# FFN input product of a transformer step by one level of Strassen's scheme, output product as a phase of its own

## The chip, the core and the metric

The kernel runs on one NeuronCore of a Trainium2 chip. The metric is the device time of one execution in microseconds. All arrays are fp32; matmuls take their operands as fp32r, and each fp32 product is made of three fp32r products.

## What is computed

One layer of a hybrid backbone for 1152 tokens (1024 latent, 128 context), D = 1024: an input projection, attention, a gated recurrence, a merge, an output projection with a gated residual, and then the gated feed-forward (FFN) part with which this case deals. Cut to that part:

```python
def conv_glu(h, w_ffn_in, conv_w, conv_b, w_ffn_out):
    T = h.shape[1]
    gate, val = jnp.split(h @ w_ffn_in, 2, axis=-1)        # 1024 x 5632
    pad = CONV_W // 2
    gp = jnp.pad(gate, ((0, 0), (pad, pad), (0, 0)))
    gconv = conv_b + sum(gp[:, j:j + T] * conv_w[j] for j in range(CONV_W))
    return (jax.nn.gelu(gconv) * val) @ w_ffn_out          # 2816 x 1024

    x = x + gt1 * (mix @ lw['w_out'])
    h2 = rmsnorm(x, lw['g_ffn']) * (1.0 + sc2) + sh2
    x = x + gt2 * conv_glu(h2, ...)
y = rmsnorm(x, g_final)
```

## The kernel before

Every operand of a product is split into `hi` (its fp32r rounding) and `lo` (the rest); a product is hi x hi + hi x lo + lo x hi, so every step of 128 in the contraction is three matmuls. ACT makes `hi` by a copy, POOL (in some places DVE) makes `lo` by a subtraction.

Only `stage_out_ffn` (L2312) changes. It writes out the queue of each engine by hand: `sync` (SP, which issues the DMAs in order), `tensor`, `scalar`, `vector`, `gpsimd`. All stages follow one another in one block, and each engine works its queue in order; semaphores join the engines.

The stage's first part is the output projection (L2654): 9 token tiles x 2 halves (`o_unit`), 24 matmuls of 512 columns a unit. Behind each tile DVE gates it (L2798), adds the residual (L2801), takes squares (L2803) and normalises (L2808); PE transposes the tile (L2666), DVE applies gain and shift (`affine`, L2818) into `y`, ACT copies to `h_hi` (L2488) and POOL makes `h_lo` (L2581). `TRANSPOSED_AFTER` says behind which unit a tile's transposes stand. `h_hi` and `h_lo` hold h2 with features on the partitions and 1152 token columns.

Then come 11 pairs (`PAIRS`) of FFN chunks of 128 channels. For each pair PE makes the gate product of both chunks, 3 banks of 384 columns each (`gate_bank`, L2674, 24 matmuls a bank), the output product of the pair before (`outs`, L2707: 18 units of 6 matmuls of 512 columns), and the value product of both chunks (`value_chunk`, L2674). ACT takes the gate out of PSUM (L2504), DVE runs the width-3 convolution over it (L2828, L2832), ACT applies gelu (L2509), DVE multiplies by the value product in PSUM (L2840), and ACT and POOL split the result `u` (L2515, L2589) into SBUF tiles that the output product reads. DVE adds each pair's output product to `yacc` in SBUF (L2850, L2853). Weights come through `WeightStream` (L116 load, L124 hi, L129 lo), w_ffn_out through `load_w2` (L2413), `w2_split` (L2527, L2595). The last two pairs' output products are kept in PSUM and joined at the end: DVE gates them with gt2 (L2895), adds `yacc` (L2908), ACT squares (L2573) and takes the root, DVE scales (L2901), SP stores (L2471).

Of the kernel before, what the change touches and what calls it, by code (L numbers as in the profile page):

```python
# [21 lines left out]
P = 128  # L22
# [2262 lines left out]
PAD = NT + 4  # L2285
LAT0, CTX0 = 1, TL + 3
WO_RING, X_RING = 2, 3
HALF = D // 2
O_UNITS = 2 * TILES
TRANSPOSED_AFTER = (6, 7, 8, 9, 11, 13, 15, 17)  # L2290


def flat_pieces(j):

    if j < 2:
        return [(LAT0 + j * CH, j * CH, CH)]
    return [(LAT0 + 2 * CH, 2 * CH, TL - 2 * CH), (CTX0, TL, TC)]


def gate_order(g):  # L2300

    if g == 0:
        return [(0, 0), (0, 1), (1, 0), (1, 1), (0, 2), (1, 2)]
    return [(x, j) for x in range(2) for j in range(NCH)]


def gate_count(g, x, j):

    return 6 * g + gate_order(g).index((x, j)) + 1


def stage_out_ffn(nc, io, cst, sems, psum, base, m_hi, m_lo, h_hi, h_lo, home, merge):  # L2312
    sems.prefix = "s8"
    after_h = base + 2 * KD * NT * 4

    first = Arena(nc, after_h)
    WO_HERE = KD // 2
# [15 lines left out]
    late = Arena(nc, after_h)  # L2333
    yacc = late("yacc", [P, TILES, D])
    over = Arena(nc, first.at)
    g_base = over.at
    gpad = [over(f"gate_pad{i}", [P, PAD]) for i in range(2)]
    conv = [over(f"conv{i}", [P, PAD]) for i in range(2)]
    w2_raw = over("w2_raw", [P, 2, D])
    gt2_once = over("gt2_once", [P, D])  # L2340
    x1_back = [over("x1_back3", [P, HALF])]
    assert over.at <= HIGH - 8
    w2_hi, w2_lo = late("w2_hi", [P, 2, D], F32R), late("w2_lo", [P, 2, D], F32R)
    u_hi, u_lo = late("u_hi", [P, 2, NT], F32R), late("u_lo", [P, 2, NT], F32R)
    x1_back = [late(f"x1_back{i}", [P, HALF]) for i in range(3)] + x1_back
    assert late.at <= first_end


    gate_home = Arena(nc, g_base)
    u0_hi, u0_lo = gate_home("u0_last_hi", [P, NT], F32R), gate_home("u0_last_lo", [P, NT], F32R)  # L2350
    assert gate_home.at <= g_base + 2 * PAD * 4
    raw_home = Arena(nc, w_base)
    w2e_hi = raw_home("w2_last_hi", [P, 2, D], F32R)
    w2e_lo0 = raw_home("w2_last_lo0", [P, D], F32R)
    raw_home("w_hi1_kept", [P, D], F32R)
    w2e_lo1 = raw_home("w2_last_lo1", [P, D], F32R)

    end = Arena(nc, base)
    u1_hi, u1_lo = end("u1_last_hi", [P, NT], F32R), end("u1_last_lo", [P, NT], F32R)
    gt2 = [end(f"gt2_row{g}", [P, D]) for g in range(2)]  # L2360
    gfin = end("g_final_row", [P, D])
    x2 = [end(f"x2_{i}", [P, D]) for i in range(3)]
    fin = [end(f"final_rows{i}", [P, D]) for i in range(3)]
    assert end.at <= after_h
# [21 lines left out]
    win = io["w_ffn_in"].rearrange("(k p) n -> p k n", p=P)
    wout = io["w_ffn_out"].rearrange("(k p) n -> p k n", p=P)
    group = lambda t: 0 if t < TILES - 1 else 1
    LAST = PAIRS - 1
    Y_PAIRS = PAIRS - 2  # L2390
    Z_TILES = (TILES - 1,) + tuple(range(TILES - 1))

    def sync(sp):
        def load_wo(k):
            n = k - WO_HERE
            if n >= WO_RING:
                sp.wait_ge(wo_lo_ready, n - WO_RING + 1)
            sp.dma_start(wo_raw[n % WO_RING][:, :], wo[k * P:(k + 1) * P, :]).then_inc(wo_loaded[n % WO_RING], 16)
# [663 lines left out]
```

## Time and profile before

| | |
|---|---|
| median of 3 runs | 2129.75 us (2128.82 to 2131.8) |
| the profiled execution | 2128.18 us, span 2126.4 us |
| granted TensorE clock, mean | 0.992 |
| PE busy | 2078.3 us (98%), 11596 matmuls |
| weight loads busy (beside PE) | 1932.5 us (91%) |
| DVE busy | 942.2 us (44%) |
| ACT busy | 650.9 us (31%) |
| POOL busy | 769.4 us (36%) |
| moved by DMA | 185.0 MB, mean 87 GB/s |

PE is TensorE, DVE VectorE, ACT ScalarE, POOL GpSimd, SP the engine that issues DMAs. Times are microseconds from the start of the span unless they are marked ns. A matmul's duration in the profile is longer than the time between two starts, since matmuls overlap; what a stream of them costs is read from starts, or from a stretch of the chain divided by its count. In a group's row stand line, engine, operation, output and inputs with their shapes, the count, busy us, the mean of one in ns, and the idle time before with what ended it.

### The profile page before, as it was taken

The numbers are of one execution on the slowest core, as the hardware profiler recorded it, in microseconds if no ns is written. First come the engines' busy times: TensorE is split into PE (matmuls) and PEld (weight loads), VectorE is DVE, ScalarE is ACT, GpSimd is POOL, SyncE is SP. The second block draws the span as 40 slices with busy tenths as digits, with TensorE's granted clock in tenths as the row PEclk, the third lists the DMA queues.
The fourth block names the chain that finished last, engine by engine and source line by source line (L and its number), as shares of the span: only waits on it lengthen the run. The fifth ranks groups of instructions, "written<-read, shape, count | busy, mean of one in ns | idle before, by whom it ended". The sixth has DMA issues, their size and how long they took to land.

```text
span 2126.4 us, 28166 instructions
## 1 busy us (share of the span) xinstructions
PE 2078.3 (98%) x11596; PEld 1932.5 (91%) x11596; DVE 942.2 (44%) x1387; ACT 650.9 (31%) x955; POOL 769.4 (36%) x512
## 2 busy tenths in 40 slices
PE   7999999999999988999999999999999999999998
PEld 6889999999999977887799879999999999999996
DVE  5326252525143046566535385235334423533556
ACT  4322323233223254767733212211121121112122
POOL 2243444434132234455536422422232232223290
PEclk9999999999999999999999999999999999999999
DMA  8754112112211375324276422211111111112132
GB/s 290 241 149 33 55 32 56 31 54 59 72 39 52 101 210 151 79 76 103 77 181 197 149 101 70 70 40 40 40 50 40 31 60 41 40 40 80 50 109 89
DMA packets 197057, 185.01 MB, mean 87 GB/s; under 512 B 55193, under 2 KB 167538, under 8 KB 196930
## 3 DMA queue, kind: packets, MB, share of 16 engines
q1 hardware_dynamic: 195634, 178.49, 28.9%
q0 software_dynamic: 1296, 4.72, 0.6%
q8 instruction: 92, 1.51, 0.3%
q14 instruction: 35, 0.29, 0.1%
HBM read 142.41 MB, written 40.78 MB: 86 GB/s over the span
## 4 chain that ended last, share of the span: by engine, by line
PE 58%; DVE 2%; DMA 2%; ACT 1%; issue 1%; SPq 0%; POOL 0%; DVEq 0%; ACTq 0%
PE late_psum L2674 26%; PE late_psum L2707 13%; PE late_psum L1849 4%; PE late_psum L1871 4%; PE late_psum L2654 4%; PE late_psum L2217 3%; PE late_psum L1819 2%; PE late_psum L1480 1%; DMA s_w_raw<-in_w_hg_o 1%; DVE p_lo L2026 0%; DMA merge_gates<-scratch_gates 0%; DVE x L2801 0%; DVE h_y L2818 0%; PE late_psum L1484 0%; ACT prob L1957 0%
## 5 line engine op out<-in xcount | busy, mean ns | idle before, releaser
L129 POOL TENSOR_TENSOR s_w_lo<-s_w_raw,s_w_hi 128x1024 fp32r<-128x1024 f32 x85 | 220.2, 2591 | 514.0 <-ACT s_w_hi L124 514.0
L2674 PE MATMUL late_psum<-h_hi,s_w_hi 128*128 128x384 f32 x1056 | 353.1, 334 | 0.7 <-ACT gate_pad L2504 0.7
L2674 PE MATMUL late_psum<-h_hi,s_w_lo 128*128 128x384 f32 x1056 | 352.9, 334 | 0.0
L2674 PE MATMUL late_psum<-h_lo,s_w_hi 128*128 128x384 f32 x1056 | 352.8, 334 | 0.0
L681 PE MATMUL s_psum<-h_hi,s_w_hi 128*128 128x384 f32 x984 | 333.2, 344 | 4.1 <-DVE h_lo L1371 4.1
L681 PE MATMUL s_psum<-h_lo,s_w_hi 128*128 128x384 f32 x984 | 326.3, 337 | 0.0
L681 PE MATMUL s_psum<-h_hi,s_w_lo 128*128 128x384 f32 x984 | 326.2, 337 | 0.0
L2674 PEld LDWEIGHTS late_psum<-h_hi,s_w_hi 128*128 128x128 f32 x1056 | 198.2, 188 | 1.5 <-issue 1.0
L2674 PEld LDWEIGHTS late_psum<-h_lo,s_w_hi 128*128 128x128 f32 x1056 | 198.2, 188 | 0.3
L2674 PEld LDWEIGHTS late_psum<-h_hi,s_w_lo 128*128 128x128 f32 x1056 | 198.2, 188 | 0.0
L681 PEld LDWEIGHTS s_psum<-h_hi,s_w_hi 128*128 128x128 f32 x984 | 185.7, 190 | 11.9 <-issue 11.7
L681 PEld LDWEIGHTS s_psum<-h_lo,s_w_hi 128*128 128x128 f32 x984 | 186.1, 190 | 0.0
L681 PEld LDWEIGHTS s_psum<-h_hi,s_w_lo 128*128 128x128 f32 x984 | 185.9, 189 | 0.0
L2853 DVE TENSOR_TENSOR yacc<-yacc,late_psum 128x512 f32<-128x512 f32 x144 | 99.1, 688 | 151.2 <-PE late_psum L2707 151.2
L2707 PE MATMUL late_psum<-w_lo,u_hi 128*128 128x512 f32 x360 | 140.4, 390 | 0.0
L2707 PE MATMUL late_psum<-w_hi,u_lo 128*128 128x512 f32 x360 | 140.2, 389 | 0.0
L2707 PE MATMUL late_psum<-w_hi,u_hi 128*128 128x512 f32 x360 | 140.0, 389 | 0.0
L2832 DVE SCALAR_TENSOR_TENSOR conv<-gate_pad,cols_b,conv 128x1154 f32<-128x1154 f32 x44 | 126.9, 2884 | 1.6
L2076 POOL TENSOR_TENSOR p_lo<-prob,p_hi 128x1024 fp32r<-128x1024 f32 x40 | 95.5, 2396 | 83.7 <-ACT p_hi L1959 83.7
L2595 POOL TENSOR_TENSOR w_lo<-w_raw,w_hi 128x2048 fp32r<-128x2048 f32 x10 | 52.7, 5270 | 194.0 <-ACT w_hi L2527 194.0
L2589 POOL TENSOR_TENSOR u_lo<-conv,u_hi 128x1024 fp32r<-128x1024 f32 (+1 forms) x40 | 57.0, 1445 | 140.0 <-ACT u_hi L2515 140.0
L954 ACT ACTIVATE sig<-s_psum 128x384 f32<-128x384 f32 x72 | 35.3, 491 | 232.9 <-PE s_psum L681 232.9
(347 smaller groups left out, 3810.4 us busy)
## 6 DMA issues: line engine op xcount, KB each, us to landing
s_w_raw<-in_w_ffn_in SPq DMA_DIRECT2D x44, 512.0 KB, 3.9
s_w_raw<-in_w_in SPq DMA_DIRECT2D x41, 512.0 KB, 4.1
s_w_mod<-in_w_mod SPq DMA_DIRECT2D x8, 2048.0 KB, 8.1
w_raw<-in_w_ffn_out SPq DMA_DIRECT2D x11, 1024.0 KB, 4.9
scratch_gates<-sig SPq DMA_DIRECT2D x48, 192.0 KB, 1.9
merge_gates<-scratch_gates SPq DMA_DIRECT2D x16, 576.0 KB, 5.0
scratch_o_mla<-o_raw SPq DMA_DIRECT2D x8, 576.0 KB, 5.1
scratch_x<-x SPq DMA_DIRECT2D x9, 512.0 KB, 2.6
```

The costliest lines, as they stand in the source:

```text
L129: pool.tensor_tensor(flat[0], flat[1], flat[2], ALU.subtract).then_inc(self.lo_ready, 1)
L681: return pe.matmul(slot_bank(s), weights(c)[wx][:, k, :], hx[:, k, j * CH:(j + 1) * CH], start=(k == 0 and n == 0), stop=(k == KD - 1 and ...
L1849: last = pe.matmul(ps_s[u % 2][:, j, :], a[e][0:QH + 1, u * P:(u + 1) * P], x[e][0:QH + 1, j * 512:(j + 1) * 512], start=(m == 0), stop=(m ...
L1871: last = pe.matmul(ps_o[:, j, :], a[e][:, u, :], x[(10 * h + u) % P_RING][:, j * 512:(j + 1) * 512], start=(u == 0 and m == 0), stop=(u == ...
L2076: pool.tensor_tensor(p_lo[(10 * h + u) % P_RING][:, :], prob[u % 2][:, :], p_hi[(10 * h + u) % P_RING][:, :], ALU.subtract).then_inc(lo_po ...
L2217: return pe.matmul(psum[c % 2][:, j, 0:CH], wx[c % 2][:, k, :], xx[half][:, k, j * CH:(j + 1) * CH], start=(k == 0 and n == 0), stop=(k == ...
L2589: last = pool.tensor_tensor(lo[:, src:src + n], conv[x][:, at:at + n], hi[:, src:src + n], ALU.subtract)
L2654: mm = pe.matmul(ps[o % 6][:, :], a[:, k, t * P:(t + 1) * P], b[k][:, half * HALF:(half + 1) * HALF], start=first and n == 0, stop=last an ...
L2674: mm = pe.matmul(ps[bank][:, 0:CH], a[s][:, k, :], b[:, k, j * CH:(j + 1) * CH], start=n == 0, stop=n == 3 * KD - 1)
L2707: mm = pe.matmul(bank[:, :], a[:, t * P:(t + 1) * P], b[:, half * HALF:(half + 1) * HALF], start=first and n == 0, stop=last and n == 3 * ...
L2832: dve.scalar_tensor_tensor(out, gpad[x][:, j:j + PAD - 2], cst.b("conv_w", 22 * j + n), out, ALU.mult, ALU.add).then_inc(conv_step, 1)
L2853: dve.tensor_tensor(dst, dst, ps[6 + n % 2][:, :], ALU.add).then_inc(y_added, 1)
```

## The change

The input product h2 @ w_ffn_in is made by one level of Strassen's scheme in Winograd's form. There are 22 "GEMMs" (`GEMMS`): for each pair of chunks one for the gate and one for the value. A GEMM's weight is cut in 2 x 2 blocks (two chunks x two halves of the contraction), h2 in 2 x 2 blocks (halves of the contraction x the two 64-column halves of every token tile). Seven products replace eight: each has four contraction steps (12 matmuls) and two parts, tiles 0 to 4 (320 columns) and 5 to 8 (256 columns), in the order 1, 2, 6, 3, 7, 4, 5.

- Operand sums of h2: POOL makes them per tile in the projection part (`make_tile`, four differences), ACT and DVE split them. For tiles 0 to 6 they go to DRAM (`store_e`) and come back after the projection (`load_extra`, six loads per part); tiles 7 and 8 are made in place, tile 8 by DVE (`combine_last`).
- Weights: raw chunks are loaded in twos, POOL makes four sums by five operations of 512 columns (`sums`), ACT makes hi and DVE makes lo (`split_weight`, 7 per GEMM) in place of POOL.
- Results: ACT copies product 1 out of PSUM (`copy`), DVE combines the others (`post`, seven additions per part with PSUM as one input) into `gpad` rows. Each part has a ring of four banks; a product waits for the post of the product four before.
- conv runs in five DVE instructions a chunk, for both chunks at the head of the value GEMM's DVE queue (`conv_gate`); the multiplication (`value`) reads SBUF only, at the head of the next GEMM.
- u goes to DRAM (`store_u`). The output product is a phase behind all GEMMs: 3 passes over three tiles, 22 steps each, 18 matmuls of 512 columns a step, accumulated in PSUM. Each step loads 128 rows of w_ffn_out (512 KB) and of u (192 KB) into one of two raw slots; ACT makes both hi, POOL w2's lo, DVE u's lo, into rings of eight. `yacc` and its additions are gone. Gate, residual, squares and scaling of a pass's three tiles stand in the queues of DVE and ACT behind the split of steps 28 and 50, and behind the last step.

```diff
-        gate_bank(0, 0, 0)
-        gate_bank(0, 0, 1)
-        transposes(TILES - 1)
-        for x, j in gate_order(0)[2:]:
-            gate_bank(0, x, j)
...
+        def strassen(i, q, b):
+            pe.wait_ge(w_lo_ready, 7 * i + ORDER.index(q) + 1)
...
+            bank_free(i, q, b)
             n = 0
+            for k in range(KB2):
+                for w, lo in ((w_hi, 0), (w_hi, 1), (w_lo, 0)):
+                    mm = pe.matmul(tiled(acc(i, q, b)), w[q][:, k, :], operand(k, q, lo, b),
+                                   start=(n == 0), stop=(n == 3 * KB2 - 1))
                     n += 1
+            mm.then_inc(product, 1)
...
+        def unit_free(p, o):
+            n = 6 * p + o
+            if n < 8:
+                pe.wait_ge(posted, count_of(GEMMS - 1, LAST_USERS[n // 2], n % 2, POSTED))
             else:
+                pe.wait_ge(e_gated, n - 7)
...
+        for i in range(GEMMS):
+            for q, b in events(i):
+                if i == 0 and (q, b) == (6, 0):
+                    transposes(TILES - 1)
+                strassen(i, q, b)
+        for p in range(PASSES):
+            tail = KO - TAIL_K if p == PASSES - 1 else KO
+            for k in range(tail):
+                step_ready(KO * p + k)
+                for o in range(6):
+                    if k == 0:
+                        unit_free(p, o)
+                    mm = end_unit(p, o, k, k == 0, k == KO - 1)
...
+        def load_step(j):
+            p, k = divmod(j, KO)
+            s = raw_slot(j)
+            if j < 2:
+                sp.wait_ge(w_lo_ready, 7 * (GEMMS - 1 + j))
+            elif j < 4:
+                sp.wait_ge(product, 14 * GEMMS)
             else:
+                sp.wait_ge(w2_lo_ready, j - 1)
+                sp.wait_ge(u_lo_ready, j - 1)
...
+        load_step(0)
+        load_step(1)
+        store_u(PAIRS - 1)
+        load_step(2)
+        load_step(3)
...
+        for i in range(GEMMS):
+            g = i // 2
+            if i % 2:
+                conv_gate(g, 0)
+            elif i >= 2:
+                value(g - 1, 0)
+                value(g - 1, 1)
+            for q, b in events(i):
+                if q in POSTED and (i, b) != (0, 0) or (i, b) == (0, 0) and q in (4, 5):
+                    post(i, q, b)
+                if b == 1 and i % 2 and q == 1:
+                    conv_gate(g, 1)
+                if b == 1 and i + 1 < GEMMS:
+                    split_weight(i + 1, q)
...
+        for j in range(2, STEPS):
+            split_step(j)
+            if j > KO and j % KO == RING2 - 2:
+                tiles = [(j // KO - 1) * PASS_TILES + t for t in range(PASS_TILES)]
+                for t in tiles:
+                    end_gate(t)
```

POOL's `sums(i + 1)` waits for the count 7 * (i + 1) of `w_lo_ready`, the last weight split of GEMM i, which DVE makes at the end of GEMM i - 1.

## Rows read from the trace of the kernel before

**Rows 1.** The page's busy line of PE, weight loads, DVE, ACT and POOL.
```profile
PE 2078.3 (98%) x11596; PEld 1932.5 (91%) x11596; DVE 942.2 (44%) x1387; ACT 650.9 (31%) x955; POOL 769.4 (36%) x512
```
**Rows 2.** The chain that ended last, in order: start, us, engine, line, count.
```profile
1918.11 49.94 PE late_psum L2674 x288
1968.05 24.52 PE late_psum L2707 x108
...
2067.53 49.47 PE late_psum L2707 x216
```
**Rows 3.** Window of the stage: length, busy by engine, clock, DMA share, GB/s.
```profile
1295.50:2126.40 830.90, 820.75 (x4365) 772.79 (x4363) 355.01 (x391) 164.57 (x239) 268.45 (x124) 1.00 0.18 56
```
**Rows 4.** Timeline of PE, matmuls of 256 columns: start, duration, what.
```profile
816.84 0.28 PE L1819 MATMUL late_psum<-ckv_hi,uk_lo 128*128 128x256 f32 x1
816.96 0.28 PE L1819 MATMUL late_psum<-ckv_hi,uk_hi 128*128 128x256 f32 x1
817.08 0.28 PE L1819 MATMUL late_psum<-ckv_lo,uk_hi 128*128 128x256 f32 x1
```
**Rows 5.** Timeline about the end of the projection, DVE.
```profile
1286.52 0.75 DVE L2808 TENSOR_SCALAR xs<-x,s_stat 128x1024 f32<-128x1024 f32 x1
...
1294.70 0.69 DVE L2798 TENSOR_TENSOR xs<-late_psum,gt_row 128x512 f32<-128x512 f32 x1 [4.28 <-PE late_psum L2654]
...
1295.42 1.23 DVE L2801 TENSOR_TENSOR x<-x,xs 128x1024 f32<-128x1024 f32 x1
```
**Rows 6.** DMA issues: count, KB each, us to landing; last the L2401 loads alone.
```profile
w_raw<-in_w_ffn_out SPq DMA_DIRECT2D x11, 1024.0 KB, 4.9
x<-in_x_sample SPq DMA_DIRECT2D x8, 512.0 KB, 3.5
...
DMA to landing us min/median/max: 3.2/3.5/7.7
```
**Rows 7.** Groups of DVE from 1290 us on, by shape.
```profile
L2840 DVE TENSOR_TENSOR conv<-late_psum,conv 128x384 f32<-128x384 f32 x44 | 23.5, 553 | 81.2 <-PE late_psum L2674 81.2
...
L2901 DVE SCALAR_TENSOR_TENSOR final_rows<-x,s_stat,g_final_row 128x1024 f32<-128x1024 f32 x9 | 11.6, 1285 | 0.3
L2908 DVE TENSOR_TENSOR x<-x,yacc 128x1024 f32<-128x1024 f32 x9 | 11.0, 1225 | 0.3
L2840 DVE TENSOR_TENSOR conv<-late_psum,conv 128x256 f32<-128x256 f32 x22 | 9.4, 426 | 68.3 <-PE late_psum L2674 68.3
```
**Rows 8.** Timelines of DVE and POOL; first conv's L2832 in ns, min/median/max.
```profile
L2832 DVE SCALAR_TENSOR_TENSOR conv<-gate_pad,cols_b,conv x44: 1420/2332/5661, 1318.9 to 2050.8; 128x1154 f32<-128x1154 f32 x44
...
1546.42 0.88 DVE L2828 TENSOR_SCALAR conv<-gate_pad,cols_b,cols_a 128x1154 f32<-128x1154 f32 x1
1547.33 7.12 DVE L2832 SCALAR_TENSOR_TENSOR conv<-gate_pad,cols_b,conv 128x1154 f32<-128x1154 f32 x2
...
1547.88 5.36 POOL L2595 TENSOR_TENSOR w_lo<-w_raw,w_hi 128x2048 fp32r<-128x2048 f32 x1 [21.55 <-ACT w_hi L2527]
```
**Rows 9.** POOL's 512 columns (min/median/max ns); POOL's 1024 and ACT's 1024 by group.
```profile
L2624 POOL TENSOR_TENSOR yacc<-yacc,x_back x18: 1287/1308/2421, 2027.4 to 2076.0; 128x512 f32<-128x512 f32 x18
...
L2598 POOL TENSOR_TENSOR w_last_lo<-w_raw,w_last_hi 128x1024 fp32r<-128x1024 f32 x1 | 2.4, 2435 | 0.0
...
L124 ACT ACTIVATE s_w_hi<-s_w_raw 128x1024 fp32r<-128x1024 f32 x42 | 44.2, 1053 | 0.0
```
**Rows 10.** A window (the clock is the third number from the end), and PE's timeline.
```profile
751.40:758.20 6.80, 5.98 (x16) 4.86 (x17) 0.69 (x1) 1.08 (x2) 0.00 (x0) 0.50 0.53 176
...
752.22 0.77 PE L1819 MATMUL late_psum<-ckv_hi,uk_hi 128*128 128x512 f32 x1 [4.22 <-PEq L88]
```
**Rows 11.** Timeline of the end: the last gate, the last store.
```profile
2117.03 0.69 DVE L2895 TENSOR_TENSOR x<-late_psum,gt_row 128x512 f32<-128x512 f32 x1 [1.55 <-PE late_psum L2707]
...
2122.03 0.33 SPq L2471 DMA_DIRECT2D out_y_prompt<-final_rows  x1
```

More of the change, by code:

```diff
@@ L2334, in stage_out_ffn @@
[L2334 to L2344, printed above, removed]
@@ L2358, in stage_out_ffn, with slot @@
[L2358 to L2364, printed above, removed]
+    extra_hi, extra_lo, w_hi, w_lo = [None] * 3, [None] * 3, {}, {}
+    def slot(arena, q):
+        w_hi[q], w_lo[q] = arena(f"ffn_w_hi{q}", [P, KB2, P], F32R), arena(f"ffn_w_lo{q}", [P, KB2, P], F32R)
@@ new lines, in stage_out_ffn @@
+    gpad = [here(f"ffn_rows{i}", [P, NT]) for i in range(2)]
+    assert here.at <= xs_at + D * 4
+    here = Arena(nc, xs_at + D * 4)
+    slot7_at = here.at
+    slot(here, 7)
+    assert here.at <= y_at
+    here = Arena(nc, y_at)
+    raw1_at = here.at
+    raw.append(here("ffn_raw1", [P, 2, KD, P]))
+    assert here.at <= gt1_at
+    slot4_at = here.at
+    slot(here, 4)
+    slot(here, 5)
+    assert here.at <= raw0_at
+    here = Arena(nc, e_at)
+    conv = [here(f"conv{i}", [P, NT]) for i in range(2)]
@@ new lines, in end_unit @@
+        def end_unit(p, o, k, first, last):
+            j = KO * p + k
+            s = step_slot(j)
+            t, half = divmod(o, 2)
+            cols = slice(half * HALF, (half + 1) * HALF)
+            n = 0
+            for a, b in ((u_hi, w2_hi), (u_lo, w2_hi), (u_hi, w2_lo)):
+                mm = pe.matmul(psum[:, pass_banks[(6 * p + o) % 8], :], a[s][:, t * P:(t + 1) * P], b[s][:, cols],
+                               start=first and n == 0, stop=last and n == 2)
+                n += 1
+            return mm
@@ new lines, in vector @@
+        value(PAIRS - 1, 0)
+        value(PAIRS - 1, 1)
+        for j in range(2, STEPS):
+            split_step(j)
+            if j > KO and j % KO == RING2 - 2:
+                tiles = [(j // KO - 1) * PASS_TILES + t for t in range(PASS_TILES)]
+                for t in tiles:
+                    end_gate(t)
+                for t in tiles:
+                    end_add(t)
+                    if t > tiles[0]:
+                        end_scale(t - 1)
+                end_scale(tiles[-1])
@@ L2905, in vector @@
+        for t in range(TILES - PASS_TILES, TILES):
             end_gate(t)
-            dve.wait_ge(e_gated, 2 * t + 2)
-            dve.wait_ge(z_ready, O_UNITS)
-            dve.tensor_tensor(x2[t % 3][:, :], x2[t % 3][:, :], yacc[:, t, :], ALU.add).then_inc(e_x2, 1)
-            if t >= 1:
+            end_add(t)
+            if t > TILES - PASS_TILES:
                 end_scale(t - 1)
```

890 lines of the change are left out of this document (539 added, 351 removed).

## The prediction

> **What bounds the kernel now.** I read the page's busy line first, then the chain that ended last in order of time, then windows over the stage, and last the single engines. PE is busy for 98% of the span [rows 1], and the chain from 1295.5 us to the end is PE alone: 288 input-product matmuls in 49.94 us, 108 output-product matmuls in 24.52 us, in turn, and 216 in 49.47 us at the end [rows 2]. So a matmul of 384 columns costs 49.94/288 = 0.1734 us and one of 512 columns 24.52/108 = 0.227 us; the 128 columns between them cost 0.0537, as 128 columns at 2.4 GHz do. The stage from 1295.5 to 2126.4 takes 830.9 us, PE busy in 820.8 of them, DVE in 355, POOL in 268 [rows 3]. PE waits for nothing there; the other engines have room. The reader is to see that only PE's stream counts today, and to ask what it costs once two other queues are filled up.
>
> **PE's own saving.** Before: 44 chunks x 3 banks x 24 = 3168 matmuls of 384 columns, 3168 x 0.1734 = 549.3 us. After: 22 half-size products ("GEMMs" in the code), each 7 products x 2 parts x 12 matmuls, half of them of 320 columns, half of 256: 1848 of each. A matmul of 256 columns starts every 0.12 us [rows 4]; 320 lies halfway to 384, (0.12 + 0.1734)/2 = 0.1467. 1848 x 0.2667 = 492.8 us. The output product keeps its 1188 matmuls of 512 columns (9 x 108 + 216 before, 66 steps x 18 after). Gain: **56.5 us**. A multiplication scheme that drops one product in eight would give 68.7; the shorter matmuls give 12 of it back. The operands now come in runs of 64 columns, which no matmul here shows; bounds 0 and, were every matmul to cost what 384 columns cost, +148 us. I take 0: the spacing of [rows 4] has the cost of streaming plus about 0.013 us, which says that streaming sets it.
>
> The Trainium skill ("TensorE: Matmul & The Clock Gate", Back-to-back issue gap) gives N/2.4 ns plus 2.5 for a warm matmul. By it the gain would be 62.0 us, as an estimate from that page; the rows have N/2.4 plus about 13, and the sum goes by them.
>
> **Start of the input product.** After the last out-product unit PE does two products (3.5 us), then transposes tile 8, which waits for DVE: gate, add, squares, normalise. In the old trace the gated half comes at 1294.70, the add at 1295.42, and normalising takes 0.75 [rows 5]; this chain ends at about 4.5 us. Now DVE also has the low part of tile 6 (3 x 256 columns, 0.9) before it and two weight splits within it, and POOL has 5.3 us of work per tile (four differences of 256, one of 1024) that it didn't have, and DVE's operations with two SBUF inputs wait for it (below). I put the transpose at 3.5 + 9. Then DVE's combining of tile 8 waits for the store of tile 6, which stands behind 3.9 MB of the first loads of the operand sums (3.9 MB at the rate of [rows 6], 1 MB in 4.9 - 2 us, is 11 us), and behind it wait DVE's split of weight 5 and h_lo of tile 8, for which PE waits: some 4 us more, and 3 at product boundaries. Price **16** (8 to 25; 8 is the chain with no POOL in its way).
>
> **DVE's queue in the value GEMMs.** Of this trace: TENSOR_TENSOR from PSUM 0.553 for 384 columns and 0.426 for 256 (1 ns a column), so 0.49 for 320; SBUF to SBUF 1.225 for 1024, so 0.72 for 512; SCALAR_TENSOR_TENSOR 1.285 for 1024, so 0.39 for 127 [rows 7]; conv's TENSOR_SCALAR 0.88 [rows 8]. Per GEMM of 7 x (1.76 + 1.44) = 22.4 us DVE has 7 x 0.92 = 6.4 of posts and 7 x 0.72 = 5.0 of splits, and every second GEMM 2 x (0.88 + 2 x 1.285 + 2 x 0.39) = 8.5 of conv, the others 2.7 of multiplying: 34 of 44.8 us per pair. That fits. But POOL has five sums of 512 columns per GEMM, 1.29 each [rows 9], and its two-input work and DVE's exclude each other: DVE's pair of conv steps, 2 x 1.42 alone, took 7.12 us while POOL's 2048-column split ran beside it, and that took 5.36 [rows 8]; 2.84 + 4.6 is the window. POOL's sums are released by the last split of the GEMM before, which is just when DVE begins conv. Walked from PE's start of a value GEMM: two posts 0.86, split 0.72, two convs 8.5, POOL's five sums between them 6.45, split 0.72, post of product 2 0.49, hand-offs 0.3: 18.0. PE's sixth product needs that post (its bank has a ring of four) and PE is there at 5 x 3.2 = 16.0. So **2 us** in each of GEMMs 3, 5, ..., 21 and, with the start's backlog, about 6 in GEMM 1: **26** (0 if POOL's sums miss the conv, 30 if each is later by 0.4).
>
> The Trainium skill ("SBUF — State Buffer") calls this an exclusive lock of a shared port pair, held for the whole instruction; by that rule, the trace agrees (7.12 for 2.84). It speaks against this change, which gives both engines more of just such work.
>
> **Turn to the output product.** Steps 0 and 1 are loaded ahead (2 x 18 x 0.227 = 8.2 us of PE). Step 2's load waits on SP behind the stores of the last two u chunks, which wait for DVE's last posts and multiplications (0.9 + 2 x 1.35 and hand-offs, 3.8 us); then 1.2 MB of stores go ahead of it in the queue, its landing (about 4.5 more than those 1.5), ACT's w2 split 1.05 and POOL's 2.4: ready at 14. Price **6** (4 to 8).
>
> **The loads of the output phase.** Each step needs 512 KB of w2 and 192 KB of u, and only two raw slots exist, so a slot's round is: landing, ACT 1.05, POOL 2.43 [rows 9], DVE's u part 0.6 after it (excluded while POOL holds the port), hand-offs 0.15. Landing: 512 KB in 3.5 (least 3.2), 1024 KB in 4.9, so 704 KB in two transfers about 3.8 (3.2 to 4.3) [rows 6]. Round 8.0, two slots: a step every **4.0 us** (3.7 to 4.25), against PE's 18 x 0.227 = 4.09. The ring of eight split steps thus never fills. That matters at a pass's turn: DVE's queue has the gating of a pass behind split 28 (and 50), while PE's step 22 (and 44) needs from its third unit on a bank that this gating frees. PE reaches it 20 x 4.09 + 1.4 = 83.2 after step 2 began; split 28 is done at 26 x 4.0, plus 2 for the nine row loads, less 1 as only u is needed: 105. Wait **22** (14 at 3.7). Then PE is six steps behind the loads, but the three tiles' gates, adds, squares and scales hold ACT and DVE some 13 us: second wait 22 x 4.0 + 13 - 22 x 4.09, **9 to 11**, I take 10 (4 to 14). In the last six steps the loads are late once more: **4** (1 to 7).
>
> **TensorE's clock.** PE had waited 4.2 us when it began again at 752.2, and 751.4 to 758.2 was granted 0.5, that is 1.2 of 2.4 GHz [rows 10]; 6 us of matmuls there did 3 us of full-clock work. Four waits here are of that length or longer: 3 us each at most, less what a slower PE gives back to late loads: **8** (0 to 14).
>
> **End.** From the last matmul's gate to the last store nothing changes by more than 0.3 us [rows 11]. The removed yacc additions (162) and final-stage z work lay beside PE and free nothing on its path.
>
> **Sum.** Against the profiled execution's 2128.2 (span 2126.4; the median of the runs is 1.6 higher): -56.5 + 16 + 26 + 6 + 22 + 10 + 4 + 8 = +35.5, so 2163.7, and by the median **2165**.
>
> **Rivals.**
> *Loads ahead of PE.* If a step is prepared in 3.1 us or less (the point where 26 steps take 81), both turns and the end wait vanish, with half the clock's term: -22 - 10 - 4 - 4 = -40, so 2123.7, by the median **2125**, faster. For it: POOL and DVE together need only 3.0 per step. Against it: it needs a landing near 2.1 us, and the least of eight landings of 512 KB is 3.2 [rows 6]. With landings of 3.2 and no late conv it comes near too: 35.5 - 26 - 8 - 6 - 3 = -7.5, **2122**. Together 0.17.
> *POOL's sums don't hold conv up.* -26: **2139**. The rows speak against it; 0.1.
> *DVE is the bound in every GEMM.* 34 of its own plus 13 of POOL's sums per pair is 47 against 44.8; if all of these exclude each other, and strided posts or hand-offs cost 2 more, each of 11 pairs takes 49 instead of the 46.9 of my sum: +23, **2188**. 0.12.
> *Runs of 64 columns slow the matmuls*, or the weight load sets their spacing: at the price of 384 columns +148 - 26 (DVE is then in time): **2287**; half of it 2226. 0.04: 256 columns at 0.12 speak against.
> *The scheme's waits chain otherwise than written*, so that PE sees few of them or many more: 0.02.
>
> **How the numbers follow.** The forecast has 0.55. The range has to take in the landing from 3.2 to 4.3 and the start's bounds, which move the sum from about +8 to +62, and the first rival's side; I take 2118 to 2200, which leaves out about 0.1 on each side. A measurement of this kernel can tell about 0.2% (4 us) from no change. Faster by more: the first rival's 0.17 and a little of the others, 0.19. Within: 0.06. Slower: 0.75.
>
> **What would show it.** Input matmuls of 320 and 256 columns starting every 0.147 and 0.120 us; conv's two-input steps on DVE stretched at the head of each value GEMM, and PE idle by about 2 us at its sixth product, released by DVE; in the last third PE waiting for DVE's first gating after step 22, 15 to 25 us, and after step 44, 5 to 14; a step's matmuls every 4.1 us before that; the clock at 0.5 behind those waits. The prediction is wrong if a step's landing is under 3 us or the ring runs full before step 22, or if matmul spacing isn't linear in columns.

## The result, and the profile after

| | before | after |
|---|---|---|
| median | 2129.76 us (2128.82 to 2131.8) | 2163.34 us (2159.28 to 2168.04) |
| the profiled execution / its span | 2128.18 / 2126.4 us | 2159.28 / 2157.5 us |
| granted clock, mean | 0.992 | 0.975 |
| first to last matmul of the projection, before tile 8's transposes | 111.2 us | 122.8 us |
| the input and output products together | 821.3 us | 513.1 + 333.4 us |
| moved by DMA | 185.0 MB | 244.2 MB |

The ratio is 1.0158 [1.0146, 1.0171]: slower by 1.6%, where 1.7% was forecast. The two profiled executions enter the projection at different times (1183.1 and 1177.9 us), and nothing of the change lies ahead of it; over all traces of this case that time runs from 1177.9 to 1187.6. From that point to the end before takes 943.3 us and after 979.6: **+36.3 us**, to be compared with the sum's +35.5.

The page's busy line after, which answers to [rows 1]:

```profile
PE 2039.6 (95%) x12124; PEld 1883.6 (87%) x12124; DVE 1228.1 (57%) x1749; ACT 741.5 (34%) x1111; POOL 894.7 (41%) x595
```

PE has 38.7 us less to do and the span is 31 us longer. Where PE stood still is read from its timeline: start, duration, what, and in brackets the idle time before it with what ended it. The twelve that carry the account (smaller ones left out):

```profile
1243.39 2.30 PE L2862 MATMUL late_psum<-ident,xs 128*128 128x128 f32 x8 [4.83 <-DVE h_y L2996]
...
1292.54 0.82 PE L2862 MATMUL late_psum<-ident,xs 128*128 128x128 f32 x4 [4.11 <-DVE h_y L2996]
...
1313.52 1.97 PE L2862 MATMUL late_psum<-ident,xs 128*128 128x128 f32 x8 [8.93 <-DVE xs L2986]
...
1324.44 0.41 PE L2892 MATMUL late_psum<-h_hi,ffn_w_hi 128*128 128x320 f32 x1 [1.29 <-DVE ffn_w_lo L3035]
...
1336.32 0.36 PE L2892 MATMUL late_psum<-extra_hi,ffn_w_hi 128*128 128x256 f32 x1 [1.70 <-DVE ffn_rows L3055]
...
1358.84 0.61 PE L2892 MATMUL late_psum<-extra_hi,ffn_w_hi 128*128 128x320 f32 x1 [3.23 <-DVE ffn_rows L3055]
...
1827.58 0.77 PE L2904 MATMUL late_psum<-w_hi,u_hi 128*128 128x512 f32 x1 [5.00 <-DVE u_lo L3097]
...
1841.07 0.47 PE L2904 MATMUL late_psum<-w_hi,u_hi 128*128 128x512 f32 x1 [2.78 <-DVE u_lo L3097]
...
1940.38 0.80 PE L2904 MATMUL late_psum<-w_hi,u_hi 128*128 128x512 f32 x1 [21.95 <-DVE x L3108]
...
2046.36 0.79 PE L2904 MATMUL late_psum<-w_hi,u_hi 128*128 128x512 f32 x1 [11.33 <-DVE x L3108]
...
2118.61 0.55 PE L2904 MATMUL late_psum<-w_hi,u_hi 128*128 128x512 f32 x1 [1.80 <-DVE u_lo L3097]
2124.01 0.76 PE L2904 MATMUL late_psum<-w_hi,u_hi 128*128 128x512 f32 x1 [4.00 <-DVE u_lo L3097]
```

The reader is to see three groups, in the projection, at the start of the input product and in the output phase, and nothing between 1358.84 and 1827.58: twenty of the 22 GEMMs run without a stop. The chain that ended last says the same of that stretch:

```profile
1358.84 455.44 PE late_psum L2892 x3408
```

455.44/3408 is 0.1336 us a matmul, half of them of 320 and half of 256 columns; the forecast was 0.1333. Some of them, in PE's timeline:

```profile
1495.12 0.28 PE L2892 MATMUL late_psum<-extra_lo,ffn_w_hi 128*128 128x256 f32 x1
1495.24 0.28 PE L2892 MATMUL late_psum<-extra_hi,ffn_w_lo 128*128 128x256 f32 x1
1495.36 0.31 PE L2892 MATMUL late_psum<-extra_hi,ffn_w_hi 128*128 128x320 f32 x1
1495.51 0.30 PE L2892 MATMUL late_psum<-extra_lo,ffn_w_hi 128*128 128x320 f32 x1
```

Starts lie 0.12 and, in the mean of the stretch, 0.147 us apart, as in [rows 4] for 256 columns: operands in runs of 64 columns cost nothing that shows.

The clock is read from windows of 10 us from the end of each wait (length, busy time of five engines, granted clock, DMA share, GB/s). Two of them, and between them the undisturbed stretch:

```profile
1358.80:1368.80 10.00, 9.96 (x55) 9.99 (x56) 7.98 (x19) 1.36 (x3) 0.00 (x0) 0.71 0.01 2
1368.80:1814.00 445.20, 445.20 (x3355) 445.20 (x3354) 375.88 (x533) 123.22 (x197) 175.52 (x97) 1.00 0.25 73
...
1940.40:1950.40 10.00, 10.00 (x34) 8.00 (x35) 8.23 (x14) 4.28 (x8) 0.00 (x0) 0.78 0.22 74
```

A mean of 0.71 over 10 us is 5.8 us at 1.2 GHz, which loses 2.9 us of full-clock work. The ten waits behind which the clock was low lose 20.2 us in this way; before has one such place (behind 1244.3, 0.83, 1.7 us).

### The profile page after: what moved, and what is told of

Read it like the earlier page. It is cut to its first block, busy times and chain, and to the rows that moved or that the text cites. A ratio compares the mean times of both kernels' runs of the same rounds, so it can differ in the third digit from the quotient of the medians.

```text
span 2157.5 us, 30841 instructions
## 1 busy us (share of the span) xinstructions
PE 2039.6 (95%) x12124; PEld 1883.6 (87%) x12124; DVE 1228.1 (57%) x1749; ACT 741.5 (34%) x1111; POOL 894.7 (41%) x595
## 4 chain that ended last, share of the span: by engine, by line
PE 41%; DVE 7%; DMA 7%; issue 3%; POOL 3%; ACT 3%; SPq 1%; DVEq 0%; ACTq 0%; POOLq 0%
PE late_psum L2892 21%; DMA u_raw<-scratch_u 5%; PE late_psum L1849 4%; PE late_psum L1871 4%; PE late_psum L2904 3%; DVE u_lo L3097 3%; PE late_psum L2217 3%; PE late_psum L1819 2%; PE late_psum L2850 1%; PE late_psum L1480 1%; DVE h_y L2996 1%; ACT u_hi L2722 1%; DMA s_w_raw<-in_w_hg_o 1%; DVE p_lo L2026 1%; POOL e_raw L2812 1%
## 5 line engine op out<-in xcount | busy, mean ns | idle before, releaser
L129 POOL TENSOR_TENSOR s_w_lo<-s_w_raw,s_w_hi 128x1024 fp32r<-128x1024 f32 x41 | 100.8, 2457 | 347.1 <-ACT s_w_hi L124 347.1
L2826 POOL TENSOR_TENSOR w_lo<-w_raw,w_hi 128x1024 fp32r<-128x1024 f32 x66 | 161.5, 2453 | 181.4 <-ACT w_hi L2717 175.2
L3097 DVE TENSOR_TENSOR u_lo<-u_raw,u_hi 128x384 fp32r<-128x384 f32 x66 | 160.3, 2438 | 121.1 <-ACT u_hi L2722 120.8
L2892 PE MATMUL late_psum<-h_hi,ffn_w_hi 128*128 128x320 f32 (+1 forms) x704 | 207.9, 295 | 2.2 <-DVE ffn_w_lo L3035 1.3
L2892 PE MATMUL late_psum<-h_lo,ffn_w_hi 128*128 128x320 f32 (+1 forms) x704 | 208.0, 295 | 0.0
L2892 PE MATMUL late_psum<-h_hi,ffn_w_lo 128*128 128x320 f32 (+1 forms) x704 | 207.9, 295 | 0.0
L2904 PE MATMUL late_psum<-w_hi,u_hi 128*128 128x512 f32 x396 | 160.9, 406 | 47.5 <-DVE x L3108 33.3
L681 PEld LDWEIGHTS s_psum<-h_hi,s_w_hi 128*128 128x128 f32 x984 | 185.0, 189 | 10.7 <-issue 10.4
L681 PEld LDWEIGHTS s_psum<-h_hi,s_w_lo 128*128 128x128 f32 x984 | 185.0, 188 | 0.0
L2892 PE MATMUL late_psum<-extra_hi,ffn_w_hi 128*128 128x320 f32 (+1 forms) x528 | 157.8, 299 | 4.9 <-DVE ffn_rows L3055 4.9
L2892 PE MATMUL late_psum<-extra_lo,ffn_w_hi 128*128 128x320 f32 (+1 forms) x528 | 157.3, 298 | 0.0
L2892 PE MATMUL late_psum<-extra_hi,ffn_w_lo 128*128 128x320 f32 (+1 forms) x528 | 157.0, 297 | 0.0
L2892 PEld LDWEIGHTS late_psum<-h_hi,ffn_w_hi 128*128 128x128 f32 x704 | 133.3, 189 | 2.9 <-DVE ffn_w_lo L3035 1.6
## 6 DMA issues: line engine op xcount, KB each, us to landing
w_raw<-in_w_ffn_out SPq DMA_DIRECT2D x66, 512.0 KB, 3.6
ffn_raw<-in_w_ffn_in SPq DMA_DIRECT2D x44, 512.0 KB, 5.2
s_w_raw<-in_w_in SPq DMA_DIRECT2D x41, 512.0 KB, 4.1
```

Source lines behind the costliest of these rows:

```text
L129: pool.tensor_tensor(flat[0], flat[1], flat[2], ALU.subtract).then_inc(self.lo_ready, 1)
L681: return pe.matmul(slot_bank(s), weights(c)[wx][:, k, :], hx[:, k, j * CH:(j + 1) * CH], start=(k == 0 and n == 0), stop=(k == KD - 1 and ...
L2826: pool.tensor_tensor(w2_lo[s][:, :], w2_raw[r][:, :], w2_hi[s][:, :], ALU.subtract).then_inc(w2_lo_ready, 1)
L2892: mm = pe.matmul(tiled(acc(i, q, b)), w[q][:, k, :], operand(k, q, lo, b), start=(n == 0), stop=(n == 3 * KB2 - 1))
L2904: mm = pe.matmul(psum[:, pass_banks[(6 * p + o) % 8], :], a[s][:, t * P:(t + 1) * P], b[s][:, cols], start=first and n == 0, stop=last and ...
L3097: dve.tensor_tensor(u_lo[s][:, :], u_raw[r][:, :], u_hi[s][:, :], ALU.subtract).then_inc(u_lo_ready, 1)
```

## Experiments

All ratios are to the kernel before. The changed kernel itself stands at 1.0158.

### The turns of the output phase: slots or something else

**Four raw slots.**

```diff
-        return j if j < 2 else 2 + (j - 2) % 2
+        return j % 4
...
-                sp.wait_ge(w2_lo_ready, j - 1)
-                sp.wait_ge(u_lo_ready, j - 1)
+                sp.wait_ge(w2_lo_ready, j - 3)
+                sp.wait_ge(u_lo_ready, j - 3)
```

> The changed kernel with four raw slots for the steps of the output product in place of two (the two places in the old weight buffers, used once so far, stay in use); nothing else moved. Theory (rate of the loads): a slot's round is 8.15 us (1890.98 to 1899.13 in the trace of the changed kernel), so two slots give a step every 4.08 us and the ring of eight never fills. With four slots the round would allow 2.0 us a step, POOL and DVE together then bind at 3.0, under PE's 4.09: the ring is full before step 22, and the waits of 21.95 and 11.33 us at steps 22 and 44, of 2.8 at step 4 and of 6.5 in the last steps go, with about 4 us of matmuls at half clock behind them. 2159.3 - 47 = 2113 us against the profiled execution, ratio to before 0.993 to 0.998. Rival (the queue's order alone: gating behind split 28 costs what it costs, whatever the loads do): the waits stay within 3 us of what they were, ratio 1.015. Rival (DMA bandwidth: more transfers in flight only land later): landing rises from 4.1 to 8 us, ratio 1.013 to 1.016.

Measured: 2116.93 us, 0.9936 [0.9921, 0.9951]. The output phase took 283.5 us in place of 333.4. PE's waits in it, from the view of waits (engine, what waited, for what: total us, times, longest), the changed kernel:

```profile
PE late_psum L2904 <- DVE x L3108: 33.3, 2, 22.0
PE late_psum L2904 <- DVE u_lo L3097: 14.3, 5, 5.0
```

and with four slots:

```profile
PE late_psum L2904 <- DVE u_lo L3097: 7.8, 2, 5.3
```

Both waits for the gating are gone, and so are those of the last six steps: 39.8 of the 49.9 us that the phase is shorter, and most of the rest is half clock behind them. The loads did not land later for being more at once: from the issue of a u load to its landing it is 3.7 us in the median with two slots, three and four, which answers the rival on bandwidth. Between two gatings DVE's `u_lo` then runs six steps in 16.2 us, 2.7 a step: the loads are paced by POOL and DVE (POOL's 2.4 and the hand-offs), no longer by the round. Once the ring is full, one step follows another in 4.12 us, PE's own pace.

**Three raw slots** (the same with `j % 3` and `j - 2`).

> As e1_four_slots, with three raw slots. Theory (the round over the slots, or POOL and DVE, whichever is longer): 8.15/3 = 2.72 us a step by the slots, 2.7 by POOL's and DVE's lo parts (six u parts in 16.19 us with four slots): both far under PE's 4.09, the ring is full before step 22, and the time is that of four slots: output phase 283 to 285 us, 2117 us, ratio 0.993 to 0.995. Rival (with three in flight the landings lengthen, and what counts is having four): steps every 3.5 us or more, a wait of 8 to 15 us at step 22, ratio 0.998 to 1.003.

Measured: 2113.38 us, 0.9933 [0.9916, 0.9949], 284.1 us for the phase. Three slots do all that four do. A round of 8.15 us over three slots is 2.7 us a step, which is already the pace that the engines set.

**Gating earlier, two slots.**

```diff
-            if j > KO and j % KO == RING2 - 2:
+            if j > KO and j % KO == 2:
```

> The changed kernel with the gating, squares and scaling of a pass's three tiles behind split 24 and 46 in DVE's and ACT's queues in place of 28 and 50; two slots as before. Theory (rate of the loads): the loads are late by themselves, with or without the gating ahead of them; the waits at steps 22 and 44 shrink to some 5 us each, but PE then starts each pass with two steps in hand in place of six and waits again at the next steps while ACT and DVE work on the three tiles. The last step is ready when it was: ratio unchanged, 1.011 to 1.017. Rival (order alone): 4 x 4.08 = 16 us less at step 22 and some 9 less at 44, nothing comes back: 2160 - 25 = 2135, ratio 1.003 to 1.006.

Measured: 2164.05 us, 1.0161 [1.0144, 1.0178]. PE's timeline at the first turn, and its waits for loads in the phase (before this edit 14.3 us in 5):

```profile
1927.18 0.80 PE L2904 MATMUL late_psum<-w_hi,u_hi 128*128 128x512 f32 x1 [4.73 <-DVE x L3108]
...
PE late_psum L2904 <- DVE u_lo L3097: 32.7, 12, 5.9
```

The two waits for the gating fall from 33.3 to 9.3 us, and most of it comes back as small ones, for loads, and as more time at half clock; the phase takes 333.1 us, 0.3 from what it took. So the place of the gating decides only where PE waits. How much it waits is set by the loads that two slots allow.

### DVE and POOL in the value GEMMs

In the changed kernel PE does not wait there from GEMM 3 on. DVE's timeline at the head of a value GEMM, and at the end its post of product 2:

```profile
1525.57 0.88 DVE L3078 TENSOR_SCALAR conv<-ffn_rows,cols_b,cols_a 128x1152 f32<-128x1152 f32 x1
1526.49 7.11 DVE L3083 SCALAR_TENSOR_TENSOR conv<-ffn_rows,cols_b,conv 128x1023 f32<-128x1023 f32 x4
1533.52 1.85 DVE L3078 TENSOR_SCALAR conv<-ffn_rows,cols_b,cols_a 128x1152 f32<-128x1152 f32 x1
1535.40 3.13 DVE L3083 SCALAR_TENSOR_TENSOR conv<-ffn_rows,cols_b,conv 128x1023 f32<-128x1023 f32 x4
...
1539.05 0.82 DVE L3055 TENSOR_TENSOR ffn_rows<-late_psum,ffn_p 128x320 f32<-128x320 f32 x2
```

and POOL's first of five sums at the same time (1.29 alone):

```profile
1525.80 1.81 POOL L2786 TENSOR_TENSOR s_raw<-ffn_raw 128x512 f32<-128x512 f32 x1 [12.99 <-DVE ffn_w_lo L3035]
```

The second chunk's four steps, alone, take 3.13 us; the first chunk's, beside POOL's sums, 7.11. The first of the two posts ends at 1539.53, and PE's sixth product, which needs it, begins at 1539.98 without a wait.

**POOL's sums behind conv.**

```diff
                     pool.wait_ge(w_lo_ready, 7 * i)
+                if i > 0 and i % 2 == 0:
+                    pool.wait_ge(conv_step, 10 * (i // 2))
```

> The changed kernel (two slots) in which POOL's five sums during a value GEMM wait until both conv steps of that GEMM are done, so that they can't hold conv up. Theory (the sums' 4.7 us of hold-up in conv are covered by the slack of 0.4 us that is left at the sixth product, except in GEMM 1, which is late from the start): the wait of 3.23 us in GEMM 1 goes, nothing else changes: -3 to -4 us, 2160, ratio 1.013 to 1.016; DVE's post of product 2 ends 4 us or more ahead of need. Rival (the hold-up is in the time of each value GEMM, as forecast): -20 us, ratio 1.006.

Measured: 2161.33 us, 1.0146 [1.0129, 1.0163]. Groups of DVE from 1368 to 1814 us, in ten value GEMMs; first the changed kernel, then this one:

```profile
L3083 DVE SCALAR_TENSOR_TENSOR conv<-ffn_rows,cols_b,conv 128x1023 f32<-128x1023 f32 x80 | 99.7, 1286 | 1.4
...
L3078 DVE TENSOR_SCALAR conv<-ffn_rows,cols_b,cols_a 128x1152 f32<-128x1152 f32 x20 | 26.3, 1316 | 0.0
```

```profile
L3085 DVE SCALAR_TENSOR_TENSOR conv<-ffn_rows,cols_b,conv 128x1023 f32<-128x1023 f32 x80 | 63.9, 841 | 1.4
...
L3080 DVE TENSOR_SCALAR conv<-ffn_rows,cols_b,cols_a 128x1152 f32<-128x1152 f32 x20 | 17.5, 876 | 0.0
```

99.7 + 26.3 - 63.9 - 17.5 = 44.6 us. All of it falls in nine of the ten: GEMM 21 is the last, so POOL has no sums to make beside it, and its conv is the same in both runs. That is 5.0 a GEMM, or 1.0 for each of POOL's five sums: the collision is real. But only GEMM 1's wait of 3.2 us went with it; the input product took 507.8 us in place of 513.1, and of this 2.8 us came back in the output phase (336.2). Most of the collision lay beside PE.

**Three more sums per GEMM**, to find how much room there was.

```diff
+                if i > 0:
+                    for c in range(3):
+                        pool.tensor_tensor(s_raw[5][:, :, :], a11, a22, ALU.add).then_inc(again, 1)
+                        pool.wait_ge(again, 3 * (i - 1) + c + 1)
                 pool.tensor_tensor(s_raw[5][:, :, :], a21, a22, ALU.add).then_inc(s_ready, 1)
```

> The changed kernel with three more sums of 512 columns on POOL in each GEMM but the first, written to a block that is overwritten after; results unchanged. In the changed kernel DVE's post of product 2 in a value GEMM ends about 0.4 us before PE's sixth product needs it (forecast: 2 us after), and the five sums (1.27 us each) stretched the conv steps by 4.7 us in all, 0.95 each. Theory (one sum costs DVE 0.95 us when it meets conv): three more make DVE 2.85 - 0.4 = 2.4 us late in each of GEMMs 3 to 21: +24 us, 2183 us, ratio 1.025 to 1.029, PE waiting for DVE at the sixth product. Rival (each costs its whole 1.27): +34 us, ratio 1.031 to 1.034. Rival (POOL doesn't hold DVE up enough to matter to PE): below +4 us, ratio 1.014 to 1.018.

Measured: 2200.41 us, 1.0325 [1.031, 1.0341]. PE at the sixth product of two successive value GEMMs:

```profile
1465.07 0.39 PE L2896 MATMUL late_psum<-extra_hi,ffn_w_hi 128*128 128x320 f32 x1 [2.46 <-DVE ffn_rows L3059]
...
1512.39 0.60 PE L2896 MATMUL late_psum<-extra_hi,ffn_w_hi 128*128 128x320 f32 x1 [2.46 <-DVE ffn_rows L3059]
```

and the windows behind them:

```profile
1465.00:1475.00 10.00, 9.93 (x74) 9.96 (x75) 10.00 (x21) 1.92 (x5) 1.62 (x1) 1.00 0.00 1
1512.30:1522.30 10.00, 9.91 (x64) 9.94 (x65) 9.12 (x20) 1.63 (x4) 0.42 (x1) 0.85 0.01 2
```

The wait is where the forecast had put it, at the sixth product and for DVE's addition, 2.46 us in nine of the GEMMs and 8.20 in GEMM 1. From the first start of conv to its last end it is 15.88 us, against 12.95 in the changed kernel: 0.98 for each of the three sums. PE's sixth product begins 18.57 us after its first, against 15.95. So 2.93 us more of DVE made PE 2.62 us late, and the changed kernel had 0.3 us of room. The waits add 27 us, against 24 expected; the ratio came out in the range of the dearer price (1.27 a sum) all the same, for another reason: behind the third, the sixth and the ninth of the nine waits the clock was low, and the input product grew by 33 us.

### The start

**Another order of the weight splits.** ACT makes the parts of weights 6 and 3 and tile 8's root ahead of tile 7's part; DVE normalises tile 8 ahead of weight 3's low part.

```diff
         split_weight(0, 6)
-        split_weight(0, 3)
         normalize(last)
+        split_weight(0, 3)
```

> The changed kernel with tile 8's chain at the start of the input product put ahead of other work: ACT makes the hi parts of weights 6 and 3 and the root of tile 8 before tile 7's copies, DVE normalises tile 8 before the lo parts of weights 3 and 7. In the changed kernel PE waited 8.93 us for tile 8's normalising (done at 1313.5; its squares were ready at 1306.1, then DVE waited 3.1 us for ACT's weight copy and 3.35 were two splits against POOL). Theory (the wait is DVE's and ACT's order): tile 8 is normalised by about 1307.8, PE's wait falls by 5 us; weights and the loads of the operand sums then allow a gain of 3 to 6 us: ratio 1.012 to 1.015. Rival (the loads of the sums or the store of tile 6 set the pace): the wait only moves behind the third or sixth product, 0 to 1 us gained, ratio 1.015 to 1.017.

Measured: 2163.96 us, 1.0157 [1.0142, 1.0173]. Two rows of its PE timeline:

```profile
1312.54 1.46 PE L2861 MATMUL late_psum<-ident,xs 128*128 128x128 f32 x8 [4.54 <-DVE xs L2985]
1325.80 0.41 PE L2891 MATMUL late_psum<-h_hi,ffn_w_hi 128*128 128x320 f32 x1 [3.35 <-DVE ffn_w_lo L3034]
```

Tile 8's wait fell from 8.93 to 4.54 us and the next one rose from 1.29 to 3.35. So the order did set that wait, as the theory has it, but half of the gain was lost again one step later, at weight 3's low part, which now stands behind the normalising. GEMM 1's wait is still 3.22, the input product is 2.4 us shorter, and the median did not move.

**Tile 7's transposes two units later** (17 in place of 16 as the last of the list).

> The changed kernel with the transposes of tile 7 behind unit 17 of the projection, where they stood before the change, in place of behind unit 16, where PE waited 4.11 us for DVE. Theory (DVE's and POOL's chain from tile to tile is what is late, PE's order only says where it is waited for): the projection's matmuls end some 4 us earlier, tile 8's normalising doesn't come earlier, the wait before its transposes grows by as much: ratio unchanged, 1.014 to 1.018. Rival (the wait belongs to PE's order): -4 us, ratio 1.012 to 1.0145.

Measured: 2165.17 us, 1.0166 [1.0151, 1.0182]. The wait of 4.11 us at 1292.54 is gone and tile 8's has grown from 8.93 to 15.30. The order of PE's queue is not what is late.

**No differences by POOL.** The projection is 11.6 us longer than before, which the forecast had put at nothing. The chain that ended last passes through one tile thus (start, us, what):

```profile
1266.48 2.65 DVE h_y L2996 x8
...
1269.20 1.39 POOL e_raw L2806
...
1270.65 0.74 POOL h_y L2808
...
1271.47 1.61 POOL e_raw L2810
...
1273.14 1.61 POOL e_raw L2812
...
1274.78 1.06 ACT h_hi L2683
1275.84 0.73 ACT e_hi L2687
1276.57 0.19 ACT s_stat L2678
...
1278.78 2.64 DVE h_y L2996 x8
```

This is a ring: DVE's affines, POOL's four differences, ACT's `h_hi` and `e_hi`, which wait for them, and behind these in ACT's queue the root of the next tile, for which DVE's next normalising and affines wait. It takes 12.3 us a tile; PE's 48 matmuls and 8 transposes take 11.96 (1258.78 to 1270.74 in the chain before).

```diff
-            pool.tensor_tensor(e[:, 1, :, :], b22, b12, ALU.subtract).then_inc(t_step, 1)
+            pool.memset(e[:, 1, :, :], 0.5).then_inc(t_step, 1)
```

(and so for two of the other three; the one in place works on a quarter of its columns).

> In the projection of the changed kernel POOL makes no full operand differences: three of the four become fills with a constant (256 columns each), the fourth works on a quarter of its columns, so that part of the computation is left out. The changed kernel's projection takes 122.8 us where the kernel before takes 111.2, and DVE's affines of successive tiles stand 12.3 us apart from tile 3 on, where PE's 48 matmuls and 8 transposes take 11.96. Theory: POOL's differences (1.3 to 1.5 us each, four a tile) exclude DVE's operations with two inputs or in SBUF and stretch DVE's chain for a tile (squares 1.54 instead of 1.22, normalise 1.58 instead of 0.75, residual 1.28), and this chain then sets the pace. Expected by it: squares at 1.22 and normalise near 0.8 again, PE's waits for affines in the projection down from 11.4 us to under 5, projection 112 to 117 us, tile 8's wait down from 8.9 by 1 to 3, ratio 1.010 to 1.013. Rival: DVE's own new work, the low part of the differences (1.18 a tile), sets the pace: projection 120 us or more, ratio 1.014 to 1.016.

Measured: 2154.43 us, 1.0111 [1.0096, 1.0126]; projection 113.4 us, waits for affines 4.6, tile 8's wait 6.17. Of DVE's groups in the projection the normalising, in the changed kernel and then here:

```profile
L2986 DVE TENSOR_SCALAR xs<-x,s_stat 128x1024 f32<-128x1024 f32 x8 | 12.6, 1581 | 0.3
```

```profile
L2986 DVE TENSOR_SCALAR xs<-x,s_stat 128x1024 f32<-128x1024 f32 x8 | 7.5, 938 | 0.3
```

The squares did not become shorter (1.75 us; they now meet POOL's `h_lo`), so that part of the expectation failed. POOL's differences, and not DVE's own low parts (1.17 us a tile, and 1.18 in the changed kernel), cost the projection its 9 to 10 us. Two things on the ring became shorter at once, POOL's part, 5.35 us down to about 1.5, and the normalising, by 0.6; 0.34 are enough to bring 12.3 under PE's 11.96, and no run tells the two apart.

### A version that is faster than both

Four slots leave the waits at steps 2 and 4. **Steps 2 and 3 loaded ahead too**: they are given slots of their own and load as soon as two splits are done, ahead of the last `store_u`; steps 4 and 5 take the place behind it.

```diff
         load_step(1)
-        store_u(PAIRS - 1)
         load_step(2)
         load_step(3)
+        store_u(PAIRS - 1)
+        load_step(4)
+        load_step(5)
```

> Four raw slots as in e1_four_slots, and the loads of steps 2 and 3 issued during the last GEMM into the two slots that steps 0 and 1 have left, ahead of the last two stores of u; steps 4 and 5 ahead of the row loads. Theory (SP's order caused the waits of 5.3 and 2.5 us at steps 2 and 4): both go, with 2 us of half clock behind them: output phase 283.5 - 10 = 274 us, 2107, ratio 0.988 to 0.990. Rival (POOL's and DVE's lo parts are what is late there, two steps after one another): only step 2's wait goes, -5 us, ratio 0.991.

Measured: 2109.74 us, 0.9907 [0.9892, 0.9922], between the theory and the rival; the output phase takes 276.1 us. The waits at steps 2 and 4 are gone, and one has come up at step 6 (2.58 us). **With POOL's sums behind conv as well:**

> The version with four raw slots and steps 2 and 3 loaded ahead of the turn, and with it POOL's sums behind the conv steps of a value GEMM. Expected: the wait of 3.2 us at GEMM 1's sixth product goes, as it did with the later sums alone (-2.0 us there), and nothing else changes: 2106 to 2109 us, ratio 0.989 to 0.990. Rival: with the output phase no longer waiting at its turns, what PE saves ahead of it comes back as a later u, and the time stays at 2109 to 2111, ratio 0.990 to 0.991.

Measured: 2104.04 us, 0.9873 [0.9857, 0.9889], a little below what was expected. The wait at GEMM 1's sixth product is gone (input product 507.0 us, 512.0 without this edit), and of it only 0.6 us come back, at step 6, where the wait was 2.58:

```profile
1844.80 0.47 PE L2913 MATMUL late_psum<-w_hi,u_hi 128*128 128x512 f32 x1 [3.20 <-DVE u_lo L3106]
```

It is 59 us faster than the change as it was made and 1.3% faster than the kernel before.

## Why the prediction was right, and where it was not

| term | forecast | measured |
|---|---|---|
| PE's own saving | -56.5 | -55.4 (3696 x 0.1336 against 549.3) |
| start of the input product | 16 | 12.0 (8.93 + 1.29 + 0.83 + 1.70, less 0.73 before) |
| projection: waits for affines | 0 | 8.0 (11.4 against 3.4) |
| value GEMMs | 26 | 3.2 |
| turn to the output product | 6 | 7.8 |
| turn 1, turn 2 | 22, 10 | 22.0, 11.3 |
| last six steps | 4 | 6.5 |
| clock | 8 | 18.5 (20.2 less 1.7 before) |
| sum | +35.5 | +33.9, of the 36.3 that the stage is longer |

The total is better than its parts. The value GEMMs were put 23 us too high, the clock 10 and the projection 8 too low, and these cancel: that the sum came within 2 us is luck. What is right by its mechanism is the saving and the output phase.

One difference stands outside the table. The output product's matmuls start every 0.229 us and in its second pass every 0.233, where [rows 2] had 0.227 and the sum took that for all of them: some 3.6 us. With four slots all passes have 0.229. Why, no run tells.

**PE's saving** held to 1 us. The Trainium skill's spacing for a warm matmul ("TensorE: Matmul & The Clock Gate", Back-to-back issue gap), N/2.4 plus 2.5 ns, would have 109 ns at 256 columns and 136 at 320; the trace above has 120 and 147. Here the row was the better guide.

**The output phase.** The load round was forecast at 8.0 us and is 8.15, from one issue into a slot to the next (1890.98 to 1899.13), or 8.25 in the mean from step 6 to step 28, here in SP's, ACT's, POOL's and DVE's timelines:

```profile
1890.98 0.33 SPq L2573 DMA_DIRECT2D w_raw<-in_w_ffn_out  x1
...
1899.13 0.33 SPq L2573 DMA_DIRECT2D w_raw<-in_w_ffn_out  x1
...
1895.11 1.06 ACT L2717 ACTIVATE w_hi<-w_raw 128x1024 fp32r<-128x1024 f32 x1 [4.05 <-DMA u_raw<-scratch_u]
...
1896.24 2.40 POOL L2826 TENSOR_TENSOR w_lo<-w_raw,w_hi 128x1024 fp32r<-128x1024 f32 x1 [3.06 <-ACT w_hi L2717]
...
1896.61 2.45 DVE L3097 TENSOR_TENSOR u_lo<-u_raw,u_hi 128x384 fp32r<-128x384 f32 x1 [3.02 <-ACT u_hi L2722]
```

4.1 us from issue to landing, 1.06 for ACT, 2.4 for POOL, and DVE's `u_lo`, 0.55 alone, which takes 2.45 because POOL runs. Slots (three, four) remove the turns' waits, and moving the gating does not: the cause named in the forecast is shown. That the first wait came out at 22.0 to the tenth is luck: PE reached the busy bank 90.9 us after step 2 began, in place of 83.2, and DVE had freed it after 112.8, in place of 105, so that both sides were late by nearly the same. The wait of 2.8 us at step 4 was not in the forecast: the load of u for it, issued just behind the nine row loads, landed after 9.1 us and not 3.7. Where steps 4 and 5 go ahead of the row loads, the late step is step 6.

**The value GEMMs** are the term that failed, 26 against 3.2. The mechanism is there (DVE's steps stretched, PE's sixth product next in line), and its size was wrong in small things that all pointed one way: a sum of POOL costs DVE 1.0 us (44.6/45) and not 1.29, five times 0.3 is 1.5; and DVE's instructions, one after another, take a little less than they do singly (split 0.61, conv of both chunks 8.0 in place of 8.5, two posts 0.75). The walk of 18.0 us measures 15.5 (1524.03 to 1539.53), and PE starts its sixth product after 15.95. A forecast 2 us over a limit was just under it, nine times; the tenth, GEMM 21, should not have been counted, since POOL has no sums there. The rival "POOL's sums don't hold conv up" gave this term nearly its right price for the wrong reason: they do hold it up, by 5.0 us a GEMM, and with three more of them PE pays.

The Trainium skill's exclusive lock of a shared port pair ("SBUF — State Buffer") is borne out in kind by these rows: `u_lo` begins 0.37 us behind POOL's instruction and ends 0.42 behind its end. For the sums it is not the whole price: POOL's five and DVE's six instructions between 1525.57 and 1535.37 come to 11.3 us of work by what each takes alone (5 x 1.29, 2 x 0.88, 3.13), done in 9.8.

**The start** was near (12 for 16), but the forecast looked only from the last unit on, and so the projection's waits stood at nothing and measure 8.0. POOL's 5.35 us a tile were in it as something that DVE runs into; that ACT's `h_hi` and `e_hi` wait for them, with the next tile's root behind, was not followed. That POOL's differences set the pace is shown by the run without them; whether by their place in the ring or by stretching DVE's normalising is not.

**The clock.** The forecast counted four waits of 4 us or more at up to 3 us each. It was ten places: a wait of 3.23 us cost 2.9 behind it, more than the 2.2 behind the wait of 22. The unit price was right and the count was not.

## What to carry to other kernels

When work is split into steps with a load each, divide the round of a slot (issue, landing, every engine that must be done with it) by the number of slots, and compare that with what the consumer needs for a step, before anything else: here 8.15/2 against 4.12 cost about 50 us, by way of two gatings in the middle of the queues and a late last few steps, and one more slot gave it back. Where a forecast says that an engine is late by a tenth of its stretch in every round, the sign of that difference isn't known from single durations; give both cases their weight. An operation added on a side engine has to be followed through the queues of all that wait for it until the ring closes, and each separate wait of PE is worth its own length plus up to 3 us of clock.

## What was not expected of the hardware

- The clock fell behind short waits, too, and not behind each: of three waits of 2.46 us of the same form, one after another (1417.8, 1465.1, 1512.4 in the run with three more sums), the windows behind show 1.00, 1.00 and 0.85, and so again with the next three and the last three. Why the third and not the others, no run here tells apart.
- DVE's TENSOR_SCALAR, with one input in SBUF, is stretched by POOL's two-input work as well: normalising 1024 columns took 1.58 us in the mean beside POOL's differences and 0.75 in [rows 5]; conv's first step 1.85 against 0.88.
- Matmul starts 0.147 and 0.12 us apart for 320 and 256 columns, against 0.1734 and 0.227 for 384 and 512, lie on one line: columns/2.4 GHz and 12 to 14 ns.
